# Packing the sample sequences and the low-rank gate into quarters of the matrix array, in a hybrid decoder step on eight cores

## What is computed

```python
a = rmsnorm(h, g_mix)
z = a @ w_in                       # q | k | v | out-gate | low-rank 16 | u | v_gmlp
log_a = log_sigmoid(alow @ w_a2 + b_a) / 16          # alow: the 16 low-rank columns
# per head (4 heads, key 128, value 256), per token:
#   S_t = diag(exp(log_a_t)) S_{t-1} + k_t^T v_t ;  o_t = q_t S_t
```

## Time and profile before

| | us |
|---|---|
| time, median of 3 runs | 1840.01 (1839.95 to 1840.67) |
| the profiled execution | 1841.19 |
| span of its slowest core (core 1) | 1839.7 |
| spans of the other cores | 1832.3 to 1837.6 |
| PE busy | 1781.4 |
| DVE busy | 791.1 |
| ACT busy | 512.4 |
| POOL busy | 137.6 |

### The profile page before, as it was taken

The page is one execution under the profiler, slowest core; times in us unless marked ns, Lnnn a source line. Parts: engine busy times, 40 slices in busy tenths (PEclk is TensorE's granted clock), DMA queues, the critical chain, the costliest instruction groups (busy, mean ns, idle before and its releaser), DMA issues.

```text
span 1839.7 us, 27107 instructions; the slowest of 8 cores (1832.3 to 1839.7 us)
## 1 busy us (share of the span) xinstructions
PE 1781.4 (97%) x10124; PEld 951.4 (52%) x10124; DVE 791.1 (43%) x1241; ACT 512.4 (28%) x925; POOL 137.6 (7%) x136
## 2 busy tenths in 40 slices
PE   5899999999999999999999999999999999999996
PEld 3465545544444566555555555555555555544442
DVE  6565525634533511333323242424241415186976
ACT  4854525745611310000000000000000000026775
POOL 1001222322000000000000000000000000000000
PEclk9899999999999999999999999999999999999998
DMA  9952487055475263434252525252424343291122
GB/s 257 228 127 69 138 190 143 12 104 125 140 141 114 44 114 64 75 57 82 51 88 46 92 47 92 47 91 47 85 54 71 68 73 69 46 183 48 62 74 81
DMA packets 42487, 171.91 MB, mean 93 GB/s; under 512 B 3188, under 2 KB 4596, under 8 KB 38520
## 3 DMA queue, kind: packets, MB, share of 16 engines
q0 software_dynamic: 28960, 108.60, 34.9%
q1 hardware_dynamic: 13112, 61.07, 9.8%
q10 hardware_dynamic: 288, 0.52, 0.1%
HBM read 259.90 MB, written 18.87 MB: 152 GB/s over the span
## 4 chain that ended last, share of the span: by engine, by line
PE 91%; DMA 3%; DVE 2%; issue 2%; ACT 2%; SPq 0%; DVEq 0%; ACTq 0%
PE pf L499 90%; DMA arena<-xp 2%; PE pb L509 2%; DVE arena L471 1%; ACT arena L461 1%; DMA arena<-g_gout 1%; DVE arena L479 0%; DVE arena L748 0%; SPq L191 0%; DVE pf L479 0%; ACT L461 0%; ACT arena L465 0%; ACT L492 0%; ACT arena L492 0%; DVE arena L494 0%
## 5 line engine op out<-in xcount | busy, mean ns | idle before, releaser
L499 PE MATMUL pf<-arena 128*128 128x512 bf16 (+4 forms) x9352 | 1737.7, 350 | 18.3 <-DVE arena L471 4.2
L499 PEld LDWEIGHTS pf<-arena 128*128 128x128 bf16 (+1 forms) x9352 | 901.4, 99 | 834.3 <-issue 35.1
L471 DVE TENSOR_TENSOR arena<-pf,arena 128x512 f32<-128x512 f32 (+3 forms) x677 | 444.7, 661 | 788.1 <-PE pf L499 734.4
L461 ACT ACTIVATE arena<-pf 128x384 bf16<-128x384 f32 (+4 forms) x310 | 160.6, 525 | 978.3 <-PE pf L499 960.0
L461 ACT ACTIVATE arena<-arena 128x512 f32<-128x512 f32 (+8 forms) x122 | 126.7, 1050 | 109.9 <-DVE arena L471 62.4
L479 DVE SCALAR_TENSOR_TENSOR arena<-arena 128x2048 bf16<-128x2048 f32 (+5 forms) x69 | 119.0, 1729 | 10.1 <-DMA arena<-g_gout 4.9
L191 POOL DMA_DIRECT2D arena<-w_f x55 | 39.0, 710 | 999.9 <-PE pf L499 970.8
L471 DVE TENSOR_TENSOR arena<-arena 128x512 f32<-128x512 f32 (+7 forms) x102 | 76.7, 762 | 50.4 <-ACT arena L461 36.2
L475 POOL TENSOR_TENSOR arena<-arena 128x1024 f32<-128x1024 f32 x31 | 72.0, 2331 | 217.7 <-ACT arena L465 126.9
L509 PE MATMUL pb<-arena 128*128 128x128 bf16 x772 | 59.6, 231 | 21.7 <-DVE arena L479 11.2
L465 ACT COPY arena<-pb 128x1024 bf16<-128x1024 bf16 (+1 forms) x54 | 53.7, 1001 | 83.8 <-PE pb L509 83.5
(11 more groups left out here) (35 smaller groups left out, 126.4 us busy)
## 6 DMA issues: line engine op xcount, KB each, us to landing
arena<-w_f POOLq DMA_DIRECT2D x44, 1024.0 KB, 9.3
arena<-w_f POOLq DMA_DIRECT2D x11, 2048.0 KB, 15.6
arena<-xm SPq DMA_DIRECT2D x18, 1024.0 KB, 11.0
arena<-w_tok POOLq DMA_DIRECT2D x8, 2048.0 KB, 23.0
arena<-xp SPq DMA_DIRECT2D x8, 1024.0 KB, 17.8
arena<-st SPq DMA_DIRECT2D x16, 512.0 KB, 4.8
sso<-arena SPq DMA_DIRECT2D x16, 512.0 KB, 3.0
arena<-w_out POOLq DMA_DIRECT2D x4, 2048.0 KB, 27.1
```

Of the source, the lines that this page charges most:

```text
L461: S.op("act", lambda: nc.scalar.activation(out=out, in_=in_, func=func, **kw), reads=reads, writes=writes, cost=c_act(n, ptr) + (0.17 if " ...
L471: S.op("dve", lambda: nc.vector.tensor_tensor(out=out, in0=a, in1=b, op=op), reads=reads, writes=writes, cost=c_dve(n, rate))
L499: ins = nc.tensor.matmul(o, lhsT=l, rhs=r, start=st, stop=sp_)
```

## The change

**Sample sequences.** They are taken in pairs, 8 steps for 16 sequences. Sequence 4j+q has its 8 tokens in partitions (and query columns) 32j to 32j+31. Step n has q = n // 2 and the two j of (0, 1) or (2, 3). For q S, the stationary operand is only the 32 columns of quarter j (of which 8 aren't zero), and the output goes to partitions 32j and on: a matmul of 128 rows by 32 columns, and the two sequences of a pair use different column quarters. For k^T v, the stationary operand has the 32 rows of quarter j by 128 columns, the moving one 32 rows of v: the two use different row quarters, and write to different banks. There are still 64 matmuls of each kind, of 256 columns. `qTm` and `ktm` are now four each, made once for each q before the steps, with `E4`, the quarters of `ET` added up. The states have four buffers instead of three. The output of the sample part, `o_s`, now lies over the first state buffer.

**Gate.** `walow2` has 16 gate columns and 16 of zero. The 16 chunks go in turn to the four column quarters, each as a matmul of 128 rows by 32 columns with 512 columns moving; each quarter adds up four chunks. ACT copies the result to `alowT`; one float32 matmul of 128 rows with `fold` adds the four quarters and repeats the sum four times; ACT adds the constant, and the rest is as before. So a call has 16 matmuls in quarters, one ACT copy and one full float32 matmul in place of 16 full matmuls, and takes six banks instead of five.

**Order.** `own_gen` begins with v tile 0, then the first decay, v tiles 1 and 2, keys and queries of the first half, the second decay, v tile 3, keys and queries of the second half, v tiles 4 to 7. `sample_gen` joins only after the fourth yield.

```diff
--- before.py
+++ after.py
@@ -24,7 +24,6 @@
 REORDER = True
 SLACK = 0.5
 TABLE = 1.3
-VF = 3
 SAMPLE_BOOST = 0.0
 LAT = 0.3
 DMA_RATE = 3.2e5
@@ -582,16 +581,24 @@
         dset(ET, BET, 1.0)
         asel(ET, BET, [[-8, 16]], 0, 1)
         asel(ET, BET, [[8, 16]], 7, -1)
-        walow4, r_ = MI.T([128, 16, 128], BF16)
-        Bwalow4 = S.buf("walow4", r_)
-        dset(walow4, Bwalow4, 0.0, 1.2)
+        walow2, r_ = MI.T([128, 16, 32], BF16)
+        Bwalow2 = S.buf("walow2", r_)
+        dset(walow2, Bwalow2, 0.0, 0.5)
         walow, r_ = RO.T([128, 16, 16], F32)
         RO.release((RO.lo, RO.hi))
         Bwalow = S.buf("walow", r_)
         S.dma("sp", walow, w_al, writes=[Bwalow], boost=8000.0)
-        for c in range(4):
-            S.op("pool", lambda: nc.gpsimd.tensor_copy(out=walow4[:, :, 32 * c:32 * c + 16], in_=walow), reads=[Bwalow], writes=[Bwalow4],
-                 cost=0.8)
+        S.op("pool", lambda: nc.gpsimd.tensor_copy(out=walow2[:, :, 0:16], in_=walow), reads=[Bwalow], writes=[Bwalow2], cost=0.8)
+        fold, r_ = MI.T([128, 4, 32], F32)
+        Bfold = S.buf("fold", r_)
+        S.op("dve", lambda: nc.vector.reduce_sum(out=fold[:, 0, :], in_=identf.rearrange("p (j r) -> p r j", j=4), axis=AX.X),
+             reads=[Bidf], writes=[Bfold], cost=0.3)
+        for c in range(1, 4):
+            DCOPY(fold[:, c, :], fold[:, 0, :], [Bfold], [Bfold], 32)
+        E4, r_ = MI.T([128, 4], F32)
+        BE4 = S.buf("E4", r_)
+        S.op("dve", lambda: nc.vector.reduce_sum(out=E4, in_=ET.rearrange("p (j q) -> p q j", j=4), axis=AX.X), reads=[BET],
+             writes=[BE4], cost=0.2)
         wa2b, r_ = MI.T([128, 128], F32)
         Bwa2 = [S.buf("wa2b", r_)]
         onec, r_ = MI.T([128, 1], F32)
@@ -733,8 +740,11 @@
 
             alowT, Balow, la, Bla = (dec or dec_p)[0:4]
             bank, Bb = nextpf()
-            o = bank[:, 0:n].rearrange("p (t j) -> p t j", j=128)
-            dense(o, lambda k: walow4[:, k, :], lambda k: aTv[:, tiles[0]:tiles[-1] + 1, k, :], 16, [Bwalow4] + Brd, [Bb], n)
+            MM([(bank[32 * (k % 4):32 * (k % 4) + 32, 0:n].rearrange("p (t j) -> p t j", j=128), walow2[:, k, :],
+                 aTv[:, tiles[0]:tiles[-1] + 1, k, :], k < 4, k >= 12) for k in range(16)], [Bwalow2] + Brd, [Bb], c_mm(16, n) / 3)
+            ACOPY(alowT[:, 0:n], bank[:, 0:n], [Bb], [Balow], n)
+            bank, Bb = nextpf()
+            MM([(bank[:, 0:n], fold.rearrange("p c r -> p (c r)"), alowT[:, 0:n], True, True)], [Bfold, Balow], [Bb], c_mm(4, n))
             ACT(alowT[:, 0:n], bank[:, 0:n], AF.Identity, [Bb, Bonec], [Balow], n, 1, bias=onec)
             bks = [nextpf() for _ in range(4)]
             MM([(bks[c][0][:, 0:n], wa2b[32 * c:32 * c + 17, :], alowT[32 * c:32 * c + 17, 0:n], True, True) for c in range(4)],
@@ -887,6 +897,11 @@
         Bvtoks = S.bufs(2, "vtoks", [r_] * 2)
         vtok, r_ = RM.T([128, 8, 1024], BF16)
         Bvtok = [S.bufs(2, "vtok%d_" % t, [part(r_, 2048 * t, 2048)] * 2) for t in range(8)]
+        qTm, BqTm = [], []
+        for i in range(2):
+            t_, r_ = RM.T([128, 4, 128], BF16)
+            qTm.append(t_)
+            BqTm.append(S.buf("qTm%d" % i, r_))
         RM.release((RM.lo, RM.hi))
 
         def kv_of(t):
@@ -983,13 +998,17 @@
 
 
         MI.r = m_kd
-        s0f, Bs0f = pair([128, 4, 256], F32, "s0f", None, "l", RO, 3)
-        qTm, BqTm = pair([128, 4, 128], BF16, "qTm", None, "l", RO)
+        s0f, Bs0f = pair([128, 4, 256], F32, "s0f", None, "l", RO, 4)
+        for i in range(2, 4):
+            t_, r_ = RO.T([128, 4, 128], BF16)
+            qTm.append(t_)
+            BqTm.append(S.buf("qTm%d" % i, r_))
+        RO.release((RO.lo, RO.hi))
         o_s, r_ = RO.T([128, 1024], F32)
         Bo_s = S.bufs(2, "o_s", [part(r_, 0, 2048), part(r_, 2048, 2048)])
         RO.release((RO.lo, RO.hi))
         s0b, Bs0b = pair([128, 4, 256], BF16, "s0b")
-        ktm, Bktm = pair([128, 512], BF16, "ktm")
+        ktm, Bktm = pair([128, 512], BF16, "ktm", None, "r", None, 4)
         attbs, r_ = MI.T([128, 4, 128], BF16, "r")
         Battbs = S.buf("attbs", r_)
 
@@ -999,29 +1018,35 @@
             ob = [nextpf(), nextpf()]
             for b_ in ob:
                 held.add(b_[1])
-            for i in range(2):
-                dset(qTm[i], BqTm[i], 0.0, 0.3)
-            S.bst = SAMPLE_BOOST
-            for i in range(16):
-                S.bst = SAMPLE_BOOST
-                sl, s3 = i % 2, i % 3
-                S.dma("sp", s0f[s3], st0[i], writes=[Bs0f[s3]])
-                ACOPY(s0b[sl], s0f[s3], [Bs0f[s3]], [Bs0b[sl]], 1024)
-                PTT(s0f[s3], s0f[s3], dsm[:, :, i:i + 1].to_broadcast([128, 4, 256]), ALU.mult, [Bs0f[s3], Bdsm], [Bs0f[s3]], 1024)
-                if i >= 2:
-                    dset(qTm[sl][:, :, 8 * (i - 2):8 * (i - 1)], BqTm[sl], 0.0, 0.15)
-                DCOPY(qTm[sl][:, :, 8 * i:8 * i + 8], qTs[:, :, 8 * i:8 * i + 8], Bq, [BqTm[sl]], 32)
-                ACT(ktm[sl], kt, AF.Copy, Bkt + [BET], [Bktm[sl]], 512, 1, scale=ET[:, i:i + 1])
-                MM([(ob[h // 2][0][:, (h % 2) * 256:(h % 2 + 1) * 256], qTm[sl][:, h, :], s0b[sl][:, h, :], i == 0 and h % 2 == 0,
-                     False) for h in range(4)], [BqTm[sl], Bs0b[sl]], [ob[0][1], ob[1][1]], 0.45)
-                bks = [nextpf(), nextpf()]
-                MM([(bks[h // 2][0][:, (h % 2) * 256:(h % 2 + 1) * 256], ktm[sl][:, h * 128:(h + 1) * 128],
-                     vt[:, h * 256:(h + 1) * 256], True, True) for h in range(4)], [Bktm[sl]] + Bvt, [bks[0][1], bks[1][1]], 0.45)
+            for q in range(4):
+                dset(qTm[q], BqTm[q], 0.0, 0.3)
+                DCOPY(qTm[q].rearrange("p h (j s) -> p h j s", j=4)[:, :, :, 8 * q:8 * q + 8],
+                      qTs.rearrange("p h (j s) -> p h j s", j=4)[:, :, :, 8 * q:8 * q + 8], Bq, [BqTm[q]], 128)
+                ACT(ktm[q], kt, AF.Copy, Bkt + [BE4], [Bktm[q]], 512, 1, scale=E4[:, q:q + 1])
+            for n_ in range(8):
+                q, jp = n_ // 2, n_ % 2
+                jj = (2 * jp, 2 * jp + 1)
+                for x, j in enumerate(jj):
+                    i, s4 = 4 * j + q, j
+                    S.dma("sp", s0f[s4], st0[i], writes=[Bs0f[s4]])
+                    ACOPY(s0b[x], s0f[s4], [Bs0f[s4]], [Bs0b[x]], 1024)
+                    PTT(s0f[s4], s0f[s4], dsm[:, :, i:i + 1].to_broadcast([128, 4, 256]), ALU.mult, [Bs0f[s4], Bdsm], [Bs0f[s4]], 1024)
+                MM([(ob[h // 2][0][32 * j:32 * j + 32, (h % 2) * 256:(h % 2 + 1) * 256], qTm[q][:, h, 32 * j:32 * j + 32],
+                     s0b[x][:, h, :], q == 0 and h % 2 == 0, False) for h in range(4) for x, j in enumerate(jj)],
+                   [BqTm[q]] + Bs0b, [ob[0][1], ob[1][1]], 0.5)
                 for hh in range(2):
-                    TT(s0f[s3][:, 2 * hh:2 * hh + 2, :], bks[hh][0][:].rearrange("p (a v) -> p a v", a=2),
-                       s0f[s3][:, 2 * hh:2 * hh + 2, :], ALU.add, [bks[hh][1], Bs0f[s3]], [Bs0f[s3]], 512)
-                S.dma("sp", sso[i], s0f[s3], reads=[Bs0f[s3]], key=Bs0f[s3])
-                S.bst = 0.0
+                    bks = [nextpf(), nextpf()]
+                    MM([(bks[x][0][:, u * 256:(u + 1) * 256], ktm[q][32 * j:32 * j + 32, (2 * hh + u) * 128:(2 * hh + u + 1) * 128],
+                         vt[32 * j:32 * j + 32, (2 * hh + u) * 256:(2 * hh + u + 1) * 256], True, True)
+                        for u in range(2) for x, j in enumerate(jj)], [Bktm[q]] + Bvt, [bks[0][1], bks[1][1]], 0.25)
+                    for x, j in enumerate(jj):
+                        TT(s0f[j][:, 2 * hh:2 * hh + 2, :], bks[x][0][:].rearrange("p (a v) -> p a v", a=2),
+                           s0f[j][:, 2 * hh:2 * hh + 2, :], ALU.add, [bks[x][1], Bs0f[j]], [Bs0f[j]], 512)
+                    if hh == 0:
+                        yield
+                        yield
+                for x, j in enumerate(jj):
+                    S.dma("sp", sso[4 * j + q], s0f[j], reads=[Bs0f[j]], key=Bs0f[j])
                 yield
                 yield
             MM([(ob[h // 2][0][:, (h % 2) * 256:(h % 2 + 1) * 256], attbs[:, h, :], vt[:, h * 256:(h + 1) * 256], False,
@@ -1032,19 +1057,24 @@
             yield
 
         def own_gen():
+            yield from v_tile(0)
             main_decay(0)
+            for t in (1, 2):
+                yield from v_tile(t)
             yield from main_kq(0)
             main_decay(1)
-            for t in range(VF):
-                yield from v_tile(t)
+            yield from v_tile(3)
             yield from main_kq(1)
-            for t in range(VF, 8):
+            for t in range(4, 8):
                 yield from v_tile(t)
 
         main_decay(2)
         run_streams(main_kq(2))
         run_streams(v_tile(8))
-        run_streams(own_gen(), sample_gen())
+        og = own_gen()
+        for n_ in range(4):
+            next(og)
+        run_streams(og, sample_gen())
```

## The result

The changed kernel is slower: 1.0085 of the kernel before (95% interval 1.0068 to 1.0101), some 15.6 us; its fastest execution took 1853.7 us. Forecast were 1828 us in a range of 1820 to 1836. The ratio rests on two executions (1853.7 and 1856.8 us), as in the other two the cores of one die ran at a lower clock.

The account below looks back on a forecast made before the run. PE was taken as the bound, busy 97% of the span. Savings of 3.0 + 1.4 + 4.0 + 4.4 = 12.8 us took 1841.2 to 1828.4, by the median 1827.2, rounded up to 1828; range 1820 to 1836.

Parts of the forecast that it names:

- Prices of the matmuls: PE matmul steps: 0.216 us for 512 columns, 0.109 for 256; a gate call's 16 in quarters 1.0 us.
- the main unknown: Whether every matmul set on quarters pays a fixed 0.13 us per pass, or only float32 weight loads do.
- rivals 1, 3 and 4: Quarter sets pay 0.13 us (1836, chance 0.13); column quarters take turns (1838, 0.10); turns plus weight loads (1858, 0.09).
- rival 4: Gate and sample matmuls: column quarters take turns and each pays its load; 18.5 us slower, 1858; chance 0.09.
- Part 3, the hole at 160 us: First decay: v tile 0 ahead closes PE's 2.7 us hole, full clock gives 1.7 more; 4.4 us saved.
- Pairs need both states loaded ... 16 us each. I take nothing: Sample part: 8 steps within 130 us leave 16 us each for states and banks; no cost counted.
- The load of the second r block ... stays hidden: Moving v tile 3 cuts this load's spare time from 15.3 to 6 us; no wait of PE.
- Part 1, "PE has v tiles and sample matmuls to do meanwhile, so nothing is taken": Gate: added ACT copy (0.58 us) hidden behind other PE work; without cover 0.6 and a wait per call, 3 us.
- Behind 300 us all is as it was, shifted: Later stages, after the sample part and r tiles: unchanged apart from the shift in time.
- The start: First 90 us, gate calls of the previous tokens: one call's saving counts once, 1.4 us (-0.6 to 2.8).
- the 12.8 us: Whole kernel: total saving forecast, from gate 3.0 and 1.4, sample sequences 4.0 and order 4.4 us.
- a microsecond of matmul taken out behind 168 us is one off the end: Stretch from 168 to 300 us: PE idle only 0.2 of 132 us, so matmul savings shorten the run fully.

Follow-up runs that it names:

- e2: The kernel before with only the new order of the v tiles, later banks put back; ratio 1.0045 to the kernel before.
- e3: The kernel before with only the gate on column quarters, padded and later banks put back; ratio 1.0083 to the kernel before.
- e6: The changed kernel with old layout and banks restored, one yield instead of two at both places of a sample step; 0.9983 of the kernel before, fastest 1837.4 us.

## Why the prediction was wrong, point by point

**Prices of the matmuls: right.** This was the main unknown, and all of rivals 1, 3 and 4 hung on it; none of the three came true, rival 4 neither, the only one that forecast a slower kernel. Two narrow windows of the changed kernel's PE timeline show matmuls on column quarters, 32 columns of weights each. The first begins a group of the sample part, the second row is a gate call, of which four start within 0.1 us:

```profile
195.37 0.28 PE L498 MATMUL pf<-arena 128*32 128x256 bf16 x2
...
201.66 0.40 PE L498 MATMUL pf<-arena 128*32 128x512 bf16 x4
```

Four matmuls of 512 columns in 0.40 us, which is one matmul's record: they start 3 ns apart. The next four follow after 0.216 us, a single matmul's step; pairs of 256 columns after 0.109 to 0.120. So the column quarters run at once and pay no fixed part. A gate call's 16 matmuls take 0.98 us with the change of mode (1.0 forecast), `fold`, where the next matmul follows it at once, 0.93 (1.07). A sample group of eight costs 0.55 us, its two groups of four on row quarters 0.32 each, 9.5 us for 8 steps (10.0 forecast). A change of mode costs 0.09 to 0.10 each way: the last transpose ahead of the group at 195.37 starts at 195.219, is 0.056 long, and the first matmul starts 0.093 behind that. The Trainium skill (TensorEngine Tiling (Array Packing), Key Properties) has the drain at such a change without a price; this is its size here. The Trainium skill (TensorE: Matmul & The Clock Gate, Measured speedup vs the span model) has 2.38 times for three column tiles. Here, in a run of matmuls, four take one matmul's step of 0.216 us, which is the full four times, and the measurement decides.

**Part 3, the hole at 160 us: right.** PE is busy 7.85 of 8 us there at clock 1.00, was 5.30 at 0.79. e2, with the order alone, has no gap there either. But from `w_q` to r its idle time falls only from 3.7 to 2.2 us, since new gaps of 0.9 to 1.0 us between matmul starts come at about 211 and 227. And the 1.7 us for the clock were there to win on two cores only: all eight had the gap of 2.9 us before, and only cores 1 and 5 show the lower level behind it.

**"Pairs need both states loaded ... 16 us each. I take nothing": wrong, and the main error.** The step compared a mean spacing of steps with nothing. It should have taken the round trip of a buffer, store and next load, from the DMA issues of the kernel before, and not the median of the whole stretch but that beside the r loads: 10.7 + 10.1 us, against 2.7 + 4.0 ahead of them. The same buffers come round every second step, and two steps of 16 us are 32 us. From these come off the trip of 20.8 us (26.2 on the chain of core 5), the cast, the product and the additions (4 us from 257.52 to 261.54), and the unevenness of the fixed order: SP issues the stores of six steps at 201.93, 223.32, 230.50, 249.17, 263.09 and 281.69 us, 7 to 21 us apart and not 16. At the hole PE was ready for the buffer at 261.54 - 5.88 = 255.66 us, 24.6 after its store went out at 231.10; the trip and the work behind it took 30.4. The waits cost 7.5 us of idle time from r to `u0`.

**"The load of the second r block ... stays hidden": right, and the wrong question.** No wait of PE for a w_tok transfer appears. I asked what the moved v tile does to the r loads, not what the r loads do to the transfers of the sample part. e2 measures the order alone: -1.5 us of idle time ahead of r, +6.5 behind, and 8.5 us of low clock.

**Part 1, "PE has v tiles and sample matmuls to do meanwhile, so nothing is taken": wrong in its size.** The price I named for the case without cover was 3 us in all. PE's order is fixed, and what lay between the gate's steps was too short: gaps between matmul starts of 1.17, 1.68 and 0.9 to 2.3 us at 201 to 210 us on all eight cores. With the low clock behind them (PEclk 0.89 over 15 us: 3.3 us at half speed, 1.7 lost) this call alone gives back its saving of 1.4. In e3 it is more: 6.4 us of idle time more from `w_q` to r.

**The clock: counted on one side only.** I took 1.7 us for the low clock that the closed hole gives back, and nothing for new holes. From `w_q` to `u0` the change has 13.6 us at the lower level (11.9 counted core by core), before has none in the median: 6 to 7 us lost, nearly as much as the idle time that came with it. Seven of e6's cores have no low clock between `w_q` and `u0`, and its gaps between matmul starts at 180 to 240 us are all of 2.0 us or less.

**"Behind 300 us all is as it was, shifted": wrong by some 3 us**, by two side effects of buffers. Both are in the kernel's text for who looks: what lies over what in the arena, and which operation gets which bank.

**The start: +0.1 us where 1.4 were forecast.** From PE's first instruction to `w_q` it is idle 27.6 us, was 23.9; the gate's saving went into waits, as the part's lower end had it. The low clock there fell from 10.2 to 3.4 us.

**What would be left of the 12.8 us.** e6 has the same matmuls and no transfer waits beside the r loads (ahead of them one stays: a load of 6.21 us on its chain at 190 us, with a gap of 1.2 us between matmul starts behind it), and gains 3 us. The rest: nothing at the start instead of 1.4; from `w_q` to r its idle time is 8.6 us, 4.9 more than before, in pieces of 1 to 2 us (gaps with ACT or DVE as releaser at 183, 212 and 231 us), at full clock. So "a microsecond of matmul taken out behind 168 us is one off the end" held for none of these kernels: with 8 us of matmul out of 255 the chains beside PE, it seems, have no slack left. The sum of these doesn't close to the microsecond; about 2 us stay unaccounted.

## What to carry to other kernels

On a bound engine with a fixed order, price the order along with the instructions: for each buffer that goes round through memory, set store + next load, read beside the traffic that will run then, against the distance of its two uses. Move the steps so that the round trips end before the large loads begin. And where a change resizes a tile or takes another bank, compare what later tiles lie over and wait for, far from the edit; a padding and a bank counter, one line each, were worth 0.44% here, more than twice what the whole change brings in its best form (0.17%).
